# Diffusion trunk on one core: normalised tiles turned one at a time, LayerNorm's weights folded into the modulation columns

## What is computed

```python
def layer_norm(x, g, b):
    x32 = x.astype(jnp.float32)
    mu = jnp.mean(x32, -1, keepdims=True)
    var = jnp.mean(jnp.square(x32 - mu), -1, keepdims=True)
    return ((x32 - mu) * lax.rsqrt(var + LN_EPS) * g + b).astype(x.dtype)
...
        hp = yp * (1 + sc_mp) + sh_mp
        hs = ys * (1 + sc_ms) + sh_ms
...
        yp = layer_norm(ALPHA * yp + g_mp * mp, ln_mix_g[i], ln_mix_b[i])
        ys = layer_norm(ALPHA * ys + g_ms * ms, ln_mix_g[i], ln_mix_b[i])
...
    aff = jax.nn.softmax((h @ router_w).astype(jnp.float32), axis=-1)
    gates, idx = lax.top_k(aff.T, cap)
    xin = h[idx]
```

## Time and profile before

| | us |
|---|---|
| median of three runs (2334.69 to 2340.25) | 2337.26 |
| the profiled execution | 2343.38 |
| its span, from the first instruction to the last | 2341.6 |
| PE busy | 2087.4 (89%) |
| DVE busy | 1840.9 (79%) |
| ACT busy | 1214.7 (52%) |
| POOL busy | 357.6 (15%) |
| all 16 DMA engines, mean rate | 240 GB/s |

### The profile page before, as it was taken

The page is one execution under the profiler, slowest core; times in us unless marked ns, Lnnn a source line. Parts: engine busy times, 40 slices in busy tenths (PEclk is TensorE's granted clock), DMA queues, the critical chain, the costliest instruction groups (busy, mean ns, idle before and its releaser), DMA issues. The chain is left out here.

```text
span 2341.6 us, 25930 instructions
## 1 busy us (share of the span) xinstructions
PE 2087.4 (89%) x10174; PEld 1450.6 (62%) x10174; DVE 1840.9 (79%) x1956; ACT 1214.7 (52%) x1483; POOL 357.6 (15%) x203
## 2 busy tenths in 40 slices
PE   6998686799999999758999999998759999999992
PEld 3554364466666666458697797886546666666661
DVE  1899886799999999745685685867769999999993
ACT  2222244577767777443444244343347777777772
POOL 1000003111111111040101101111410110111113
PEclk9998888899999999978899998999779999999996
DMA  7466503899999999821024132251359999999992
GB/s 284 162 248 278 229 36 144 282 375 377 391 381 374 391 386 379 308 71 55 0 91 99 54 78 58 90 135 40 138 175 370 377 382 388 377 377 394 376 354 95
DMA packets 81178, 561.81 MB, mean 240 GB/s; under 512 B 9377, under 2 KB 9393, under 8 KB 24993
## 3 DMA queue, kind: packets, MB, share of 16 engines
q1 hardware_dynamic: 66976, 508.81, 56.4%
q0 software_dynamic: 14080, 51.34, 8.5%
HBM read 523.94 MB, written 36.18 MB: 239 GB/s over the span
## 5 line engine op out<-in xcount | busy, mean ns | idle before, releaser
L1661 DVE TENSOR_TENSOR w_l<-ring,w_h 128x2048 fp32r<-128x2048 f32 x384 | 869.5, 2286 | 38.2 <-ACT w_h L1143 35.8
L1143 ACT ACTIVATE w_h<-ring 128x2048 fp32r<-128x2048 f32 x384 | 736.1, 1919 | 270.8 <-PE bank L649 270.1
L647 PE MATMUL bank<-w_h,xin_h 128*80 128x512 f32 x1024 | 408.7, 399 | 2.5 <-DVE xin_l L1681 1.3
L648 PE MATMUL bank<-w_l,xin_h 128*80 128x512 f32 x1024 | 404.1, 395 | 0.0
L649 PE MATMUL bank<-w_h,xin_l 128*80 128x512 f32 x1024 | 401.1, 392 | 0.0
L1417 POOL DMA_INDIRECT z_rows<-hT,slot_i x32 | 101.1, 3160 | 950.2 <-DVE hT L1692 950.2
L647 PE MATMUL bank<-w_h,hidT_h 128*80 128x512 f32 x512 | 205.5, 401 | 5.7 <-DVE hidT_l L1675 5.7
L647 PEld LDWEIGHTS bank<-w_h,xin_h 128*80 128x80 f32 x1024 | 152.2, 149 | 93.4 <-DVE xin_l L1681 10.4
L649 PEld LDWEIGHTS bank<-w_h,xin_l 128*80 128x80 f32 x1024 | 152.4, 149 | 86.3 <-issue 1.6
L649 PE MATMUL bank<-w_h,hidT_l 128*80 128x512 f32 x512 | 201.0, 393 | 0.0
L648 PE MATMUL bank<-w_l,hidT_h 128*80 128x512 f32 x512 | 200.5, 392 | 0.0
(11 more groups left out here) (273 smaller groups left out, 3375.7 us busy)
## 6 DMA issues: line engine op xcount, KB each, us to landing
ring<-w_stream SPq DMA_DIRECT2D x396, 1024.0 KB, 7.9
ring<-w_stream SPq DMA_DIRECT2D x38, 2048.0 KB, 9.5
z_rows<-X POOLq DMA_DIRECT2D x15, 512.0 KB, 8.3
X<-z_rows SPq DMA_DIRECT2D x15, 512.0 KB, 5.4
h_rows<-scr POOLq DMA_DIRECT2D x10, 512.0 KB, 4.0
ln_gb<-ln_rows POOLq DMA_DIRECT2D x4, 1024.0 KB, 6.8
X<-x_in SPq DMA_DIRECT2D x2, 1280.0 KB, 17.7
y_out<-X SPq DMA_DIRECT2D x5, 512.0 KB, 2.7
```

The lines of the kernel that those rows point to most:

```text
L647: pe.matmul(out[0:SLOTS, :], ah[:, c, :], wh[:, k, :], start=(first and k == 0), stop=False)
L648: pe.matmul(out[0:SLOTS, :], ah[:, c, :], wl[:, k, :], start=False, stop=False)
L1143: A(w_h[m % NB][:, :, :], src, ACT.Copy).then_inc(s["high_ready"], 1)
L1661: V.tensor_tensor(w_l[m % NB][:, :, :], src, w_h[m % NB][:, :, :].bitcast(F32), ALU.subtract)\
```

## The change

LayerNorm's multiplication by `g` and addition of `b` are taken out of the way of the next sub-layer. Since h = (n * g + b) * scale + shift for a normalised row n, the columns become scale * g and shift + b * scale, once for each sub-layer (`fold_ln`, on DVE). What is turned is n itself:

- `turn(b, t)` turns one tile as soon as it is normalised, eight transposes into a pair of banks. ACT evacuates chunks 0 to 3 and DVE chunks 4 to 7, with the folded columns (`turn_evac`).
- The router's product is formed per tile with the tokens on the output's partition (`logits(t)`, 128x16), which takes the copy and the turning back away. The time products are formed per tile as well (`dt_part`).
- POOL's two instructions per tile remain (`x_final`), since the residual path needs n * g + b; they stand behind the last turn, and ahead of the stores to `z_rows`. Ahead of the scan they work on a copy `xn` and wait until the low part of `hT` is complete.
- The high and low parts ahead of the scan are formed per tile (`hT_split`, `hT_rest`); the gate's columns and the first two weight splits move ahead of the normalisation.
- The rows' stores to `h_rows` are issued by ACT in place of POOL.
- The output is written turned, from `hT`, with columns for the last LayerNorm; POOL takes no part in it. A store then has 8 runs of 512 bytes for each partition, where it had one of 4 KB.

```diff
+        def turn_cols(b, k, t):
+
+            if b == 2 * DEPTH:
+                o = 2 * KC * (b - 1) + k
+                return ln_c[:, o:o + 1], ln_c[:, o + KC:o + KC + 1]
+            L, sh, c = b // 2, shift_part(b), int(t == NS)
+            return mT[:, L, sh + 8 + k, c:c + 1], mT[:, L, sh + k, c:c + 1]
+
+        def turned(b, k, t):
+
+            return bank[turn_pair(b, t)[k // 4]][:, (k % 4) * P:(k % 4 + 1) * P]
...
-                sp.wait_ge(s["x_ready"], 15 + t + 1)
-                sp.dma_start(y_out[:, t, :], X[:, t, :]).then_inc(s["y_stored"], 16)
+                n = turn_n(2 * DEPTH, t)
+                sp.wait_ge(s["turn_a"], 4 * (n + 1))
+                sp.wait_ge(s["turn_v"], 4 * (n + 1))
+                sp.dma_start(y_out[:, :, t * P:(t + 1) * P], hT[:, :, t * P:(t + 1) * P]).then_inc(s["y_stored"], 16)
...
-            def build_hT(b, behind=None):
-
-                pe.wait_ge(s["x_ready"], 5 * b)
+            def turn(b, t):
+
+                n = turn_n(b, t)
+                pe.wait_ge(s["ln_normed"], n + 1)
...
+                src = xn if b == 2 else X
                 for k in range(KC):
-                    if k >= 2:
-                        pe.wait_ge(s["hTs_ready"], 8 * b + k - 1)
-                        pe.wait_ge(s["hTp_ready"], 8 * b + k - 1)
-                    for t in range(NT):
-                        out = bank[k % 2][:, t * P:(t + 1) * P] if t < NS else bank[2 + k % 2][:, 0:P]
-                        ins = pe.transpose(out, X[:, t, k * P:(k + 1) * P], ident)
-                    ins.then_inc(s["hT_tr"], 1)
-                    if behind and k >= 2:
-                        behind(k - 2)
-                if behind:
-                    hT_whole(b)
-                    behind(KC - 2)
-                    behind(KC - 1)
+                    ins = pe.transpose(turned(b, k, t), src[:, t, k * P:(k + 1) * P], ident)
+                    if k % 4 == 3:
+                        ins.then_inc(s["turn_mm"], 1)
...
+                def logits(t):
+
+                    turned_wait(b, t)
+                    if L == 1 and t == 0:
+                        pe.wait_ge(s["out_added"], 10 * GROUPS - 3)
+                    for k in range(KC):
+                        ins = pe.matmul(bank[(6, 2)[L]][:, t * EXPERTS:(t + 1) * EXPERTS], hT[:, k, t * P:(t + 1) * P],
+                                        wr[:, L, k, :], start=(k == 0), stop=(k == KC - 1))
+                    ins.then_inc(s["logits_mm"], 1)
...
+                turn(b, 0)
+                for t in range(1, NT):
+                    turn(b, t)
+                    logits(t - 1)
+                logits(NT - 1)
...
+            def dt_part(t):
+
+                turned_wait(2, t)
+                for k in range(KC):
+                    ins = pe.matmul(bank[3][:, t * 64:(t + 1) * 64], hT[:, k, t * P:(t + 1) * P], wdt[:, k, :],
+                                    start=(k == 0), stop=(k == KC - 1))
+                ins.then_inc(s["dtr_mm"], 1)
...
+            turn(2, 0)
+            for t in range(1, NT):
+                turn(2, t)
+                dt_part(t - 1)
+            dt_part(NT - 1)
...
+            def turn_evac(b, t):
+
+                n = turn_n(b, t)
+                if t == 0:
+                    act.wait_ge(s["fold_ready"], 1)
+                act.wait_ge(s["turn_mm"], 2 * n + 1)
+                for k in range(4):
+                    scale, bias = turn_cols(b, k, t)
+                    A(hT[:, k, t * P:(t + 1) * P], turned(b, k, t), ACT.Identity, bias=bias, scale=scale)\
+                        .then_inc(s["turn_a"], 1)
...
+                    if h == 1:
+                        act.wait_ge(s["hback_ready"], 10 * L + n + 1)
+                        act.dma_start(h_rows[t * P:(t + 1) * P, :], rows[t]).then_inc(s["rows_stored"], 16)
...
+            def hT_split(t):
+
+                act.wait_ge(s["ln_normed"], 2 * NT)
+                act.wait_ge(s["turn_a"], 4 * (turn_n(2, t) + 1))
+                act.wait_ge(s["turn_v"], 4 * (turn_n(2, t) + 1))
+                c = slice(t * P, (t + 1) * P)
+                A(hT_h[:, :, c], hT[:, :, c], ACT.Copy).then_inc(s["hT_high"], 1)
...
+            gate_evac(2, 0)
+            normalise(1, 0)
+            normalise(1, 1)
+            for t in range(2, NT):
+                turn_evac(2, t - 2)
+                normalise(1, t)
+            turn_evac(2, 3)
+            for t in range(3):
+                hT_split(t)
+            turn_evac(2, NS)
+            hT_split(3)
+            hT_split(NS)
...
+            for t in range(3):
+                normalise(2, t)
+            for t in range(3, NT):
+                turn_evac(3, t - 3)
+                normalise(2, t)
+            for t in range(2, NT):
+                turn_evac(3, t)
...
+            def x_final(b):
+
+                pool.wait_ge(s["ln_loaded"], 16 * b)
+                src = xn if b == 2 else X
+                if b == 2:
+                    pool.wait_ge(s["hT_low"], NT)
+                pool.wait_ge(s["turn_mm"], 2 * (turn_n(b, NS) + 1))
                 for t in range(NT):
-                    if t < NT - 1:
-                        pool.wait_ge(s["ln_normed"], NT * b + t + 1)
-                        pool_step(nc.gpsimd.tensor_tensor(X[:, t, :], X[:, t, :], ln_gb[:, 0, :], ALU.mult))
-                        pool_step.sync()
-                    else:
-                        pool.wait_ge(s["ln_scaled"], b + 1)
-                    nc.gpsimd.tensor_tensor(X[:, t, :], X[:, t, :], ln_gb[:, 1, :], ALU.add).then_inc(s["x_ready"], 1)
...
+                x_final(2)
                 x_store(2)
...
+            def fold_ln():
+
+                part = st[:, :, :, :].rearrange("p a b c -> p (a b c)")[:, 0:2 * KC]\
+                    .rearrange("p (k c) -> p k c", c=2)
+                for b in range(1, 2 * DEPTH):
+                    L, sh, o = b // 2, shift_part(b), 2 * KC * (b - 1)
+                    g, c = [ln_c[:, i:i + KC].rearrange("p (k c) -> p k c", c=1).broadcast_to([P, KC, 2])
+                            for i in (o, o + KC)]
+                    scale, bias = mT[:, L, sh + 8:sh + 16, :], mT[:, L, sh:sh + 8, :]
+                    link(V.tensor_tensor(part, scale, c, ALU.mult))
+                    step(V.tensor_tensor(bias, bias, part, ALU.add))
+                    ins = V.tensor_tensor(scale, scale, g, ALU.mult)
+                    if b < 2 * DEPTH - 1:
+                        link(ins)
+                    else:
+                        link(ins)
+                        V.tensor_copy(part[:, 0, :], part[:, 0, :]).then_inc(s["fold_ready"], 1)
...
+            wx_rest(0, 0)
+            wx_rest(0, 1)
+            turned_stats(1, 0)
+            turned_stats(1, 1)
+            for t in range(2, NT):
+                turned_stats(1, t)
+                turn_evac(2, t - 2)
+            turn_evac(2, 3)
+            hT_rest(0)
+            hT_rest(1)
+            turn_evac(2, NS)
+            for t in range(2, NT):
+                hT_rest(t)
...
+                        if t == 3:
+                            turn_evac(3, 0)
+                            turn_evac(3, 1)
+                for t in range(2, NT):
+                    turn_evac(3, t)
```

More of the change, by code:

```diff
@@ L225, in build @@
         Y = take("ssd", NT, GC)
+        at["ssd"] -= NT * GC
+        wdt = take("ssd", KC, 64)
+        at["ssd"] += NT * GC - KC * 64
         Btok = take("ssd", NT, P)
@@ L247, in build @@
         Em = take("ssd", 4, TOK)
-        at["ssd"] = mark + NT * GC
-        wdt = take("ssd", KC, 64)
+        at["ssd"] = mark
+        xn = take("ssd", NT, D)
         at["ssd"] = mark
@@ L696, in moe, with rows_back @@
                 pe.wait_ge(s["wr_loaded"], 16)
[L698 to L712, removed]
-                for t in range(NT):
-                    out = bank[5][0:EXPERTS, t * P:(t + 1) * P] if t < NS else bank[6][0:EXPERTS, 0:P]
-                    ins = pe.transpose(out, aff[:, t, :], ident)
-                ins.then_inc(s["aff_tr"], 1)
-                for n in range(2 * NT):
+                def logits(t):
[6 more added lines that the diff above has]
+                    ins.then_inc(s["logits_mm"], 1)
+                def rows_back(n):
                     t, h = n // 2, n % 2
@@ L723, in moe @@
                     ins.then_inc(s["hback_tr"], 1)
+                turn(b, 0)
[3 more added lines that the diff above has]
+                logits(NT - 1)
+                pe.wait_ge(s["aff_ready"], L + 1)
+                for t in range(NT):
+                    out = bank[5][0:EXPERTS, t * P:(t + 1) * P] if t < NS else bank[7][0:EXPERTS, 0:P]
+                    ins = pe.transpose(out, aff[:, t, :], ident)
+                ins.then_inc(s["aff_tr"], 1)
+                for n in range(2 * NT):
+                    rows_back(n)
                 pe.wait_ge(s["hback_ready"], 10 * L + 10)
@@ L766, in ssd_project @@
                 for k in range(KC):
-                    if i == 0:
```

(41 more changed lines are left out.)

166 lines of the change are left out of this document (74 added, 92 removed).

## The result

The changed kernel takes 2308.36 us (median of four runs, 2302.43 to 2312.33), the kernel before 2338.76 beside it: 0.9876 of it, with a 95% interval of 0.9858 to 0.9894, or 30.4 us less. The forecast was 2304 and 33.5 less. The sum came out nearly right, but three of its four terms did not: two gained less than forecast and one more.

The account below looks back on a forecast made before the run. Most of the span was put in the two expert stages, PE busy almost throughout, which the change leaves alone. Four passages between stages gain 6.7 + 7.2 + 12.4 + 7.2 = 33.5 us: 2337.3 - 33.5 = 2304, range 2286 to 2318.

Parts of the forecast that it names:

- A: Router of the first expert stage: gather at 404 and not 412.7, 8.7 us, less 2 for the queue: 6.7 us.
- 5 x 1.83 + 3 x 1.24 = 12.9: First router: PE's five products and three turns in series at the higher clock, 12.9 us, softmax at 379.0.
- C: Second router: gather at 1714.0 against 1727.42, 13.4 us, less 1 for the queue: 12.4 us.
- The queue behind the stores: Both routers: the gather stands behind the stores in POOL's queue; 2 us (0 to 6.3) and 1 us (0 to 5) taken off.
- rival 3: Both routers: the gather's data waits for the stores ahead; first router gives 2.4, second 7.5, time 2313 us; chance 0.15.
- B: Entry to the scan: third projection at 1050.4 us, 7.2 us earlier, with the softplus chain waiting for POOL's ten instructions.
- T: Entry to the scan: the time, 1017.5 us, at which the first projection can start and POOL starts its ten instructions.
- rival 1: Entry to the scan: POOL does not hold the softplus chain; gain there 25.7 us, time 2285 us; chance 0.12.
- rival 2: Both routers: the top-k's instructions wait for POOL too, slots 12.8 and 8.2 us late, time 2344 us; chance 0.08.
- D: Output: ACT ends at 2324.0 against POOL's 2332.75, 8.75 us, less 1.5 for shorter store runs: 7.2 us.
- 2324.0 against POOL's 2332.75: Output: end of ACT's evacuations and the last turn against the end of POOL's work before, 8.75 us.
- The fold: Ten column instructions on DVE ahead of the residual loop, 2.4 us, costing nothing under PE's products.

Follow-up runs that it names:

- e5: Changed kernel with extra wide products, read by nobody, ahead of each tile's 16-column router products: 2306.3 us, 0.9882 of the kernel before.
- e1: Changed kernel with both routers' weights loaded and the turned tile streamed (128 columns), result turned back: 2297.59 us, 0.9845 of the kernel before.
- e9: e8 plus POOL's scan-entry instructions waiting only for each tile's own turn, and six unread 256-column products in each router's gap: 2283.6 us, 0.9771.
- e8: e1 with the first gather issued ahead of the five stores to z_rows and the load of the next LayerNorm weights: 2294.3 us, 0.9819.
- e4: Changed kernel with POOL's ten scan-entry instructions and the five stores behind them held until the fifth projection is done: 2307.44 us, 0.9889.
- e6: Changed kernel plus one unread POOL multiplication of 128x1024 behind the output's last turn: 2310.87 us, 0.9887 of the kernel before.
- e7: The kernel before, unchanged, run again for a second trace: 2335.67 us, 0.9999.

## Why the prediction was right, and where not

- **A: 6.7 forecast, nothing won.** The step that failed is "PE stands still only 2 us before this, so I use the higher clock". The stretch ran at 0.50, and "5 x 1.83 + 3 x 1.24 = 12.9" took 22.0 us (366.42 to 388.4). The unit costs were right for the higher clock: e5's rows give 1.85 and 1.07, and the same stretch takes 13.9 us in e1, where only the tile behind the pause is slow, and 12.3 in e9, where the pause is filled too. So of the 9 us lost the pause (3.13 us, not 2) is worth some 1.6 and the form of the products the rest. The row that I took the costs from the earlier trace rows streams 64 columns, the router's products 16; of the clock I asked only how long PE had stood still, not what products so narrow would do to it. Softmax to slots took 24.2 us with the one wait for POOL (1.49) that was counted, and POOL's ten instructions took 24.0 as counted.
- **C: 12.4 forecast, 8 to 11 won.** The same step: the softmax came 23.7 us after the last product and not 18.2. The way to the third tile's products was as counted (11.6 us, forecast 11.4); the three products and the turn behind it, put at 6.7, took 12.0.
- **The queue behind the stores** was put at 2 and 1 us. It cost 0.9 in A, where the late slots left the stores 3.8 us to get ahead, and 0.2 in C. As soon as the slots are early (e1) it costs 4 to 5 in A and still nothing in C: rival 3 is a real mechanism in A that the slow clock hid, within the 0 to 6.3 that I had given it. Its 2.6 MB leave out the load of the next weights, 1 MB more, which e1 and e8 point at. In its sum C's 7.5 should be 8.4 (13.4 less 5), which makes its time 2312.
- **B: 7.2 forecast, 9.0 won.** Right in its steps: T was 1018.45 (1017.5), of the chain's instructions beside POOL's ten each but RECIPROCAL waited, and e4 shows what rival 1 would have had, a chain of 9.3 us. The row of one-operand statistics pointed the other way; the multiplications and the copy waited (2.27, 2.43), RECIPROCAL did not (2.15 with POOL, 2.16 in e4). PE's idle time of some 18 us came out at 13.4: the first projection's first 6 us ran at 0.50, which cost nothing there. The Trainium skill's page "SBUF — State Buffer", section "Who interferes with whom", names copies and multiplications by a constant among the instructions that can contend in this way and leaves other one-operand ones free; the trace agrees, with the 0.69 us of MAX8 beside POOL for the other half. Those 0.69 us are also why rival 2 did not come.
- **D: 7.2 forecast, 12.7 won.** The evacuations were right (17.7 us, forecast 17.4), and the stores took 0.8 us more each where 1.5 was counted: up to the last landing D won 6.9 (28.8 to 21.9). What was mis-sized is the end of the kernel before: I set "2324.0 against POOL's 2332.75" and left out that the program ended 8.85 us behind POOL's last instruction, not with the last landing (2335.4; e6's expectation has 2335.8). e6 and e7 show that this tail goes with POOL.
- **The fold** cost nothing that shows: the last product of the convolution module ends between 359.9 and 363.5 in eight traces with the change, at 359.6 and 361.4 in two without.
- **The sum** was near by luck: A and C came out 7.5 and 1.5 to 4.2 below the forecast, B and D 1.8 and 5.5 above it. Of the marks, four named the softmax and the slots (379, 1689, 404, 1714): 388.5 and 412.7 in A, and, with C's 20.1 us of earlier start added, 1694.6 and 1718.8. They alone would have told the failed step; the total would not.

## What to carry to other kernels

A duration taken from another stage's row carries that stage's clock with it: when products are recast, ask what the engine will do around them, and read the granted clock of the nearest stretch that looks like it. Here 80 passes took nearly twice what the row had promised, with PE busy all the time. When POOL's work is moved off one chain, list which instructions of DVE it will then lie beside, and move it to where these are few: the same ten instructions held DVE up by 18 us behind the low parts and by some 16 beside the convolutions, and spread over the turns they made the first projection about 7 later. Ahead of a first gather, look at what stands on its queue: clearing it was worth 5.6 us in A, and nothing in C, where only stores were moved.

## What was not expected of the hardware

- TensorE's granted clock fell from 1.00 to 0.50 within a stretch in which the engine paused for no more than 0.63 us, when only 16-column products and 128-column turns were left (C, 1655.9). It stayed up there in e1, where products of 128 columns took their place, and in e5, where products of 256 stood between, until a pause of 3.43 and 2.05 us.
- The program ends 8.1 to 8.85 us behind POOL's last instruction where that comes late (before, e6, e7); where POOL's last instruction was 30 us before the end (2270.3 of 2300.6 in the changed kernel) it ends with the last landing.
- A gather of 80 rows took 8.9 us from issue to first use with nothing ahead of it on POOL's queue, 14.5 with 3.6 MB (five stores and the load of the weights) issued 1.3 us ahead, and 8.5 with the stores alone (2.6 MB) issued 2.2 us ahead (e1).
